# A diffusion step's expert stage on one core: one loop body for all sixteen experts, and a pass ahead of them that jumps over the body

## What is computed

```python
aff = jax.nn.softmax((h @ w_router).astype(jnp.float32), axis=-1)
gate, idx = lax.top_k(aff.transpose(0, 2, 1), cap)        # 64 latent and 16 context tokens for each expert
xs = jax.vmap(lambda hb, ib: hb[ib])(h, idx)
a = jnp.einsum('becd,edf->becf', xs, w1)
b = jnp.einsum('becd,edf->becf', xs, w3)
y = jnp.einsum('becf,efd->becd', jax.nn.silu(a) * b, w2) * gate[..., None]
```

## Time and profile before

| | us |
|---|---|
| median of 3 runs | 2695.71 |
| lowest and highest of them | 2691.11, 2699.36 |
| the profiled execution: its time | 2696.3 |
| its span in the trace | 2694.5 |
| experts of layer 0, from PE's first block to the end of its last | 865.6 to 1338.3 |
| experts of layer 1 | 2186.9 to 2661.3 |
| PE busy, share of the span | 94% |

### The profile page before, as it was taken

The page is one execution under the profiler, slowest core; times in us unless marked ns, Lnnn a source line. Parts: engine busy times, 40 slices in busy tenths (PEclk is TensorE's granted clock), DMA queues, the critical chain, the costliest instruction groups (busy, mean ns, idle before and its releaser), DMA issues.

```text
span 2694.5 us, 79955 instructions
## 1 busy us (share of the span) xinstructions
PE 2520.7 (94%) x31456; PEld 1918.2 (71%) x31456; DVE 1164.1 (43%) x2031; ACT 814.8 (30%) x3454; POOL 961.5 (36%) x2976
## 2 busy tenths in 40 slices
PE   6999999999997999999889999999999969999995
PEld 3555676666755899888746566766666559988885
DVE  3998534555426111111278874345644341111114
ACT  3112223434214343333021132334331143433320
POOL 2374223232201255445535632133221014554444
PEclk9999999999999999999999999999999979999998
DMA  8332311112336899999723322111242249999993
GB/s 329 114 146 94 113 60 50 67 63 103 148 125 256 327 427 428 427 427 427 331 102 125 132 95 92 61 66 53 105 167 74 113 159 404 427 427 427 428 427 148
DMA packets 45134, 572.39 MB, mean 212 GB/s; under 512 B 5248, under 2 KB 7424, under 8 KB 9600
## 3 DMA queue, kind: packets, MB, share of 16 engines
q1 hardware_dynamic: 42336, 553.67, 50.7%
q10 hardware_dynamic: 2592, 16.38, 1.5%
HBM read 561.11 MB, written 8.91 MB: 212 GB/s over the span
## 4 chain that ended last, share of the span: by engine, by line
PE 67%; DMA 20%; DVE 10%; issue 2%; ACT 1%; DVEq 0%; POOL 0%; POOLq 0%; ACTq 0%
PE ps L511 50%; DMA ring<-in_w_exp 18%; PE ps L678 6%; DVE region_b L1707 5%; PE ps L933 3%; DMA ring<-in_w_last 2%; PE ps L899 1%; PE ps L882 1%; PE ps L870 1%; PE ps L1043 1%; DVE region_r L1996 1%; DVE rstd L1621 0%; DVE region_r L1995 0%; DVE region_r L1999 0%; PE ps L785 0%
## 5 line engine op out<-in xcount | busy, mean ns | idle before, releaser
L2321 POOL TENSOR_TENSOR region_m<-region_m,region_r 128x8 f32 x2416 | 424.1, 217 | 542.8 <-DVE region_r L2036 489.3
L511 PE MATMUL ps<-hT,ring 128*128 128x320 f32 (+2 forms) x1440 | 429.0, 440 | 8.4 <-ACT hT L1221 8.2
L2329 ACT ACTIVATE region_b<-hT 128x8 f32 x2400 | 290.6, 204 | 270.4 <-DVE region_r L2049 158.9
L511 PEld LDWEIGHTS ps<-hT,ring 128*128 128x128 f32 x1440 | 256.2, 191 | 145.0 <-issue 65.7
L511 PE MATMUL ps<-region_r,ring 128*64 128x80 f32 x7812 | 287.3, 233 | 22.2 <-DMA ring<-in_w_exp 19.3
L511 PEld LDWEIGHTS ps<-region_r,ring 128*64 128x64 f32 x7812 | 278.3, 137 | 28.9 <-DMA ring<-in_w_exp 25.8
L1707 DVE SCALAR_TENSOR_TENSOR region_b<-region_b,params 128x655 f32<-128x655 f32 x240 | 277.6, 1157 | 8.5
L511 PE MATMUL ps<-region_b,ring 128*128 128x320 f32 (+1 forms) x812 | 191.7, 373 | 0.5 <-DMA ring<-in_w_last 0.5
L511 PE MATMUL ps<-region_r,spare 128*64 128x80 f32 x4032 | 152.6, 237 | 27.9 <-DVE region_r L2331 18.1
L2167 POOL TENSOR_TENSOR params<-ring 128x512 f32<-128x512 f32 x32 | 41.9, 1310 | 372.2 <-DMA ring<-in_w_pair 370.7
L511 PEld LDWEIGHTS ps<-region_r,spare 128*64 128x64 f32 x4032 | 147.7, 140 | 32.0 <-DVE region_r L2331 18.6
(11 more groups left out here) (291 smaller groups left out, 3778.8 us busy)
## 6 DMA issues: line engine op xcount, KB each, us to landing
region_b<-in_w_exp SPq DMA_DIRECT2D x60, 2048.0 KB, 25.2
ring<-in_w_exp SPq DMA_DIRECT2D x60, 2048.0 KB, 25.3
ring<-in_w_mix SPq DMA_DIRECT2D x39, 2048.0 KB, 8.1
region_x<-in_w_exp SPq DMA_DIRECT2D x30, 2048.0 KB, 25.2
spare<-in_w_exp SPq DMA_DIRECT2D x30, 2048.0 KB, 25.3
ring<-in_w_pair SPq DMA_DIRECT2D x32, 1536.0 KB, 6.4
ring<-in_w_ada SPq DMA_DIRECT2D x4, 2048.0 KB, 10.3
x_store<-region_m ACTq DMA_DIRECT2D x2, 2560.0 KB, 10.6
```

Of the source, the lines that this page charges most:

```text
L511: ins = pe.matmul(*args, **kw)
L2321: last = eng.tensor_tensor(x[:, :, token], x[:, :, token], y_gated[e % 2][:, :, c:c + 1], ALU.add)
L2329: last = eng.activation(into[:, :, c:c + 1], h[:, :, token], ACT.Copy)
```

## The change

The loop body becomes one expert: w1, w3, w1, w3, w2, w2 of the same expert, blocks 6e to 6e+5, with six slots (4, 1, 5, 2, 3, 0) from the first block on. The blocks written out ahead of the loop and behind it are gone. `pe.Fori(0, NE + 1)` makes seventeen passes, and each block stands in a `pe.If(e)` of its own: in the pass e = 0 PE jumps over all six. The wait for `xs_first` is inside the first of them. In w2 half 0, PE takes the first half of the rows of all four column groups before it waits for the second product of silu and b. y has two banks. The gates are laid and spread for one expert at a time, by a matmul in each pass. ACT gathers 48 columns ahead of `silu(2e)` and 32 after it. DVE finds the context tokens ahead of its last latent round, so that after the last result 8 columns are left to gather (ACT 3, POOL 2, DVE 3) and 16 are gathered before. PE does all of `next_ada` ahead of `turn_affinities(2)`. The four `in_w_ada` blocks go to slots 7, 6, 3 and 0 and are issued at the pairs 11 to 13 and behind `br_read`, where blocks of experts were. DVE no longer helps with expert 14. Cut to its core:

```diff
-FIRST_BLOCKS, LOOP_BLOCKS, LAST_BLOCKS = 4, 3 * (HALVES - 2), 2
...
-ADA_SLOTS = (0, 1, 2, 0)
-FIRST_SLOTS = (7, 3, 6, 0)
-LOOP_SLOTS = (4, 1, 5, 2, 7, 3)
-AHEAD = 8
+ADA_SLOTS = (7, 6, 3, 0)
+EXP_SLOTS = (4, 1, 5, 2, 3, 0)
...
-        take(FIRST_SLOTS[_n] if _n < FIRST_BLOCKS else LOOP_SLOTS[(_n - FIRST_BLOCKS) % EXP_BLOCKS], expert=(_l, _n))
+        take(EXP_SLOTS[_n % EXP_BLOCKS], expert=(_l, _n))
...
-        GATE_BANKS = [(PS[1][:, 1, 0:6 * CAP], 0, 6), (PS[3][:, 0, 0:6 * CAP], 6, 6), (PS[3][:, 1, 0:4 * CAP], 12, 4)]
-        gates_laid = sq[0:NE, 0:NE * CAP].rearrange("p (e c) -> p e c", e=NE)
+        gates_laid = sq[0:NE, 0:CAP]
+        a_ps, b_ps = PS[0][:, 0, 0:HC], PS[0][:, 1, 0:HC]
+        y_banks, gate_bank = [PS[1][:, 0, 0:HC], PS[2][:, 0, 0:HC]], PS[1][:, 1, 0:CAP]
...
-                    if (name, p) == ("pair", 11):
-                        load_expert(0)
-                    if (name, p) == ("pair", 12):
+                    if l == 0 and (name, p) == ("pair", 11):
+                        load_next_ada(0)
+                    if l == 0 and (name, p) == ("pair", 12):
                         need("o_ready", 2 * PAIRS)
                         sp.wait_ge(kv_stored, 2 * 16 * (l + 1))
-                        load_expert(2)
+                        load_next_ada(1)
                     if (name, p) == ("pair", 13):
                         need("br_step", 56)
-                        load_expert(1)
+                        load_next_ada(2) if l == 0 else load_expert(4)
                     if (l, n) == (0, 0):
                         sp.dma_start(first_block, a["w_conv0"]).then_inc(first_in, 16)
                 need("br_read", 32)
-                load_expert(4)
+                load_expert(0)
+                load_next_ada(3) if l == 0 else load_expert(5)
+                load_expert(1)
+                need("ctx_out_done", 2)
+                load_expert(2)
+                load_expert(3)
                 if l == 0:
-                    for n, b in enumerate(NEXT_ADA[:SLOTS]):
-                        load(BLOCK_AT[1][b], a["w_ada"][n])
-                else:
-                    load_expert(3)
+                    load_expert(4)
                     load_expert(5)
-                need("ctx_out_done", 2)
-                load_expert(6)
-                if l == 0:
-                    for at, b in enumerate(NEXT_ADA[SLOTS:], SLOTS):
-                        load(BLOCK_AT[1][b], a["w_ada"][at])
-                    load_expert(5)
-                load_expert(7)
-                if l == 0:
-                    load_expert(3)
-                for n in range(AHEAD, EXP_BLOCKS * NE):
+                for n in range(EXP_BLOCKS, EXP_BLOCKS * NE):
...
+                        if m == 0 and pending:
+                            last.then_inc(slot_used[pending.pop(0)], 1)
...
-                next_ada(("turn", 1), ("rows", 2))
+                next_ada(("turn", 1), ("rows", 2), ("turn", 2), ("rows", 3), ("turn", 3))
                 turn_affinities(2)
-                next_ada(("turn", 2), ("rows", 3), ("turn", 3))
-                a_ps, b_ps = PS[0][:, 0, 0:HC], PS[0][:, 1, 0:HC]
-                y_ps = PS[1][:, 0, 0:HC]
...
+                def spread_gates(e):
+                    need("gates_laid", e)
+                    pe.matmul(gate_bank, ones[0:NE, :], gates_laid, start=True, stop=True).then_inc(S["gates_wide"], 1)
+                def expert_step(w, ps, moving, m, k, start):
+                    for at in range(0, P, WCOLS):
+                        ins = pe.matmul(
+                            ps[at:at + WCOLS, m * CAP:(m + 1) * CAP],
+                            w[:, k, m * P + at:m * P + at + WCOLS], moving[:, k, :],
+                            start=start, stop=k == KC - 1, tile_position=(0, at), skip_group_check=True)
+                    return ins
+                def up_block(n, turns, ps, done):
                     w = weights(EXP_AT[l] + n, turns)
                     for m in range(4):
                         for k in range(KC):
...
+                            ins = expert_step(w, ps, xs, m, k, k == 0)
                     ins.then_inc(S[done], 1)
...
-                need("xs_first", 3)
-                up_blocks(0, 0, 0, True)
-                spread_gates()
-                up_blocks(1, 2, 0, False)
-                with pe.Fori(1, NE) as e:
-                    need("xs_ready", e)
-                    up_blocks(2 * e, FIRST_BLOCKS, e - 1, False)
-                    down_block(2 * e, FIRST_BLOCKS + 2, e - 1)
-                    up_blocks(2 * e + 1, FIRST_BLOCKS + 3, e - 1, False)
-                    down_block(2 * e + 1, FIRST_BLOCKS + 5, e - 1)
-                for b in range(LAST_BLOCKS):
-                    need("act_ready", HALVES)
-                    expert_block(FIRST_BLOCKS + LOOP_BLOCKS + b, 0, last_banks[b], act_last, "y_done")
...
+                def down_block(n, e, half):
+                    w = weights(EXP_AT[l] + n, e - 1)
+                    need("y_copied", 2 * e + half)
+                    for part in range(2):
+                        if part and not half:
+                            need("b_used", 2 * e + 2)
+                        for m in range(4):
+                            for k in range(part * KC // 2, (part + 1) * KC // 2):
+                                ins = expert_step(w, y_banks[half], act, m, k, (m, k) == (0, 0))
+                    ins.then_inc(S["y_done"], 1)
+                assert not pending
+                if l + 1 < LAYERS:
+                    pe.wait_ge(S["ada_part_in"], ADA_BLOCKS * (l + 1) + ADA_EARLY[l + 1])
+                with pe.Fori(0, NE + 1) as e:
+                    for half in range(2):
+                        with pe.If(e):
+                            if half == 0:
+                                need("xs_first", 3)
+                                need("xs_ready", e)
+                            need("sil_ready", 2 * e + half)
+                            up_block(2 * half, e - 1, a_ps, "a_done")
+                        with pe.If(e):
+                            need("b_used", 2 * e + half)
+                            up_block(2 * half + 1, e - 1, b_ps, "b_done")
+                    for half in range(2):
+                        with pe.If(e):
+                            if half == 0:
+                                spread_gates(e)
+                            down_block(4 + half, e, half)
...
+                need("index_ready", 8)
+                take_slots(nc, sc, mybir.EngineType.Activation, index, 0, h, xs, CAPL, CAPL + 8)
                 need("index_ready", 9)
-                take_slots(nc, sc, mybir.EngineType.Activation, index, 0, h, xs, CAPL, CAPL + 5).then_inc(S["xs_first"], 1)
+                take_slots(nc, sc, mybir.EngineType.Activation, index, 0, h, xs, CAPL - 8, CAPL - 5).then_inc(S["xs_first"], 1)
                 def silu(i):
                     need("a_done", i + 1)
                     if i >= 2:
-                        need("act_ready", i // 2 * 2)
-                    sc.activation(sil[i % 2], PS[0][:, 0, 0:HC], ACT.Silu).then_inc(S["sil_ready"], 1)
+                        need("b_used", i + 1)
+                    sc.activation(sil[i % 2], a_ps, ACT.Silu).then_inc(S["sil_ready"], 1)
                 def next_slots(e, c0, c1):
-                    if e < NE:
-                        return take_slots(nc, sc, mybir.EngineType.Activation, index, e, h, xs_next, c0, c1)
...
-                for e in range(1, NE):
+                    return take_slots(nc, sc, mybir.EngineType.Activation, index, e, h, xs_next, c0, c1)
+                sc.sem_inc(S["sil_ready"], 2)
+                for e in range(NE):
                     if e < NE - 1:
-                        need("xs_ready", e)
-                        next_slots(e + 1, 0, CAP // 2)
+                        if e:
+                            need("xs_ready", e + 1)
+                        next_slots(e + 1, 0, PARKED)
                     silu(2 * e)
                     if e < NE - 1:
-                        next_slots(e + 1, CAP // 2, CAP).then_inc(S["xs_parked"], 1)
+                        next_slots(e + 1, PARKED, CAP).then_inc(S["xs_parked"], 1)
                     silu(2 * e + 1)
...
+                    if c == CAPL - 8:
+                        need("aff_turned", 2)
+                        link(v.tensor_copy(affW[:, LAT:TOK], PS[2][0:NE, 1, 0:CTX]), "aff_copied")
+                        for ctx_c in range(CAPL, CAP, 8):
+                            top(ctx_c, CAPL, LAT, TOK, CAPC)
+                        link(v.tensor_scalar(best_raw[:, CAPL:CAP], best_raw[:, CAPL:CAP], float(LAT), None, ALU.add),
+                             "index_ready")
                     top(c, 0, 0, LAT, CAPL)
...
+                take_slots(nc, v, mybir.EngineType.DVE, index, 0, h, xs, CAPL - 3, CAPL).then_inc(S["xs_first"], 1)
+                def lay_gates(e):
+                    if e:
+                        need("gates_wide", e)
```

(65 more changed lines are left out.)

83 lines of the change are left out of this document (15 added, 68 removed).

## The result

| | us |
|---|---|
| before, median of 4 runs | 2696.38 |
| after, median of 4 runs (lowest, highest) | 2822.31 (2817.48, 2826.27) |
| ratio, with its 95% interval | 1.0468 (1.0445 to 1.0492) |
| span of the profiled execution, before and after | 2694.5, 2820.2 |

What follows compares the result with a forecast made beforehand. The experts' weight stream, 5.04 us per block, and its start bound the kernel. Layer 0's +9.7 and layer 1's +1.4 sum to +11.1 us: 2707.4 against the profiled 2696.3, 0.6 less against the median, 2707; range 2680 to 2717.

Steps and rivals of the forecast that it cites:

- the jump pass and the stream: Both expert loops: fetches put first blocks at 879.0 and 2193.7; block 6's issue to last start 457.1 us; sum +11.1 us.
- No stall of over 1 us: Sign of being right: in the expert loops' first pass of work, no "issue" pauses of over 1 us.
- what a fetch costs: Jump pass: five packets waited for per layer, one behind the other, 3.8 us each, 4.5 for layer 0's first.
- the old body of six blocks stays held; the new one is longer by some tens of instructions: PE's expert loop: argument against code being fetched again in every pass, which would cost 400 us in all.
- rival 3: Expert loop body outgrows what PE holds: every pass fetches again, 13 us per pass, 400 us in all; chance 0.04.
- The rule of the skill: Jump pass: prefetch is sequential only; a taken branch to a block not held forces a fetch before execution goes on.
- The shorter wait for the first block: Ahead of the experts: fewer columns left to gather, 0.9 us, starts 864.6 and 2186.0 without the jump; worth nothing behind it.

Runs made afterwards that it cites:

- e1: The changed kernel with 40 long-met waits (about 20 PE instructions) ahead of layer 1's loop, so its body lies in seven packets: 2706.95 us, ratio 1.0038.
- e2: The kernel before with 472 long-met waits (236 instructions) ahead of layer 1's experts, moving its loop's head to a packet's end: 2753.32 us, ratio 1.021.
- e5: The changed kernel with 74 more wait instructions ahead of layer 0's loop, so layer 0's body touches eight packets and layer 1's seven: 2846.94 us, ratio 1.0599.
- e7: The changed kernel with 56 more wait instructions ahead of layer 0's loop, both bodies in seven packets, layer 0's ending near its seventh's end: 2704.99 us, ratio 1.0036.
- e8: The changed kernel without the empty first pass and jumps, layer 1's body kept where it touches eight packets: 2795.44 us, ratio 1.0364.
- e3: The changed kernel without the empty first pass and jumps, layer 1's loop moved by 20 instructions into seven packets: 2693.38 us, ratio 0.999.
- e4: The changed kernel with three jumps over pairs of blocks instead of six, layer 1's loop moved by 20 instructions: 2700.08 us, ratio 1.0024.
- e6: The changed kernel with layer 1's loop moved by 40 waits and a second empty pass added in layer 1: 2710.26 us, ratio 1.0052.

## Why the prediction was wrong, step by step

**Right in kind and size: the jump pass and the stream.** From block 6's issue, at 882.37 in the SP timeline, to the last start of layer 0, 1339.44, it is 457.07 us; forecast 457.1. No stall of over 1 us is left in layer 0's first pass. PE comes to its pass 2.7 us earlier than I had it, since all of this execution ahead of the experts was 2.7 us earlier than in the profile before; from there to the first block it is 19.5 us, and my sum had 20.0. e1, the change with the misplacing taken out, has 2706.95 against the forecast's 2707: layer 0 starts its first and last block at 878.26 and 1342.43 (forecast 879.0, 1343.4), and layer 1's last block starts at 2668.19, where 2658.1 and layer 0's 9.7 make 2667.8.

**Right by errors that cancel: what a fetch costs.** I had five fetches of 3.8 us in each layer. q8 has six packets in layer 0's pause, at 859.7, 862.9, 866.2, 869.4, 872.4 and 875.4, one each 3.2 us and not 3.8; the last starts 0.4 us ahead of the first block, less than the 0.94 that a packet takes, so five seem to be waited for. The first starts 3.4 us behind PE's arrival, where I had at most 1.2, and that makes up for the cheaper ones. Layer 1 of e1 has seven, 2184.8 to 2204.3, and by the same reading waits for six: 21.8 us for my 19.3, while PE came there 1.3 us earlier than forecast and the stretch to the last block was 0.8 shorter. I had counted blocks; what counts is the packets that the body touches, less what is held on arrival. In the kernel after, layer 1's pause is 27.4 us with nine packets, 2183.2 to 2207.3: there the body is lost for the first time as soon as PE jumps back from the pass that only fetched it.

**Failed: "the old body of six blocks stays held; the new one is longer by some tens of instructions", so 0.04 for rival 3, and it was left out of the range.** So the sum gave refetching nothing, and it is 115 of the 126 us. The step asked whether the body's length fits. What decides is how many packets it touches, and that is its length and its place: 1560 instructions are seven packets from slot 172 and eight from slot 250. The 15 instructions that the body grew by weren't needed for it: e2's old body, moved, is lost too. The earlier trace rows showed a loop that is held; they couldn't show with how much to spare, and I read a "yes" as a margin. Nor did I ask for each layer by itself, though the two loops are compiled to two places. e1, e5, e7 and e8 show it with the same body in both places, and e2 with the old body. Rival 3's price per pass that fetches, 13 us against 13.5, came out right by luck: it was seven packets of 6.2 us against 30 us of work, and it is nine packets and a pause of 11.8 to 13.4 us at the back edge. Its count was wrong: eight such passes, in one layer, and not all of both.

By the sum of the parts: the stretch ahead of the first block of layer 1 is 22.9 us later than before (2209.78 against 2186.92), of which 8.0 are there already at the last matmul ahead (2181.99 against 2173.98); from there to the last block's start another 103.7 (573.5 against 469.8): together 126.5, less 0.8 behind it: 125.7, the difference of the spans.

**The rule of the skill.** The Trainium skill, "Runtime: NRT & Kernel Launch", section "Instruction fetch mechanics", was right that a jump to a packet not held waits for it. The same section gives TensorE a buffer of 128 KiB in blocks of 16 KiB, which makes eight blocks. Runs here agree with it as an order of size, and put the edge at seven packets touched. That the eighth is kept for the packet fetched ahead would explain it. The packet that starts 0.3 to 0.4 us ahead of the first block (in both layers of e1 and in layer 0 of the kernel after), too late to be waited for, and the nine packets of each refetch, one more than the body touches, fit that; no run tests it. The Trainium skill, "Advanced Engine Details and Errata", section "ISA Cache", with its two lines, doesn't hold for PE in this kernel: seven stay held through a layer.

**Not settled**: why only every second pass fetches (every fourth or second in e2, at times two in a row in e5), and why the pause at the back edge, 11.8 to 13.4 us, is two fetches long (7.3 and 4.4 us in e5) while further packets of the same pass cost 0.3 to 2 us each. One reading is that those come ahead of PE while it works and compete with the weights.

**A better version.** None. e3 is at 0.999 with an interval up to 1.0: within what a measurement of this kernel can tell from no change. The shorter wait for the first block that the rest of the change brings (863.11 against 865.55) is paid for by a block at the lower clock, 7.23 us against 5.89, and the stalls stay.

## What to carry to other kernels

A hardware loop whose body comes near to what its engine holds has to be judged by the packets it touches in the compiled program, for each copy of the loop: a few instructions ahead of it can be worth 4% of the time (e1 against the kernel after), and every timing of a change to such a kernel is then a timing of its placement too. So look first at whether q8 has packets in the later passes of each layer, and if it has, move the loop by some idle instructions before anything else is concluded. A pass that only fetches code pays one fetch after another, 3.2 us a packet here, and is worth it only where PE is idle for that long anyway.

## What the runs showed of the hardware that I had not expected

- PE keeps seven packets of 16 KB through sixteen passes (q8 has none in 340 us), and with eight touched it loses them all, nine packets for each refetch: 45 packets in 390 us, 13.5 us per pair of passes. The step from one to the other is 18 instructions or fewer (e7 against e5), 14 in e8 against e3.
- Code that is jumped over by pairs of packets is fetched all the same (e4: 68 packets, no stall in the first pass of work).
- A pass of six jumps over held code isn't free: 2.7 us (e6).
- After a pause at the back edge the next block runs 5.9 to 7.5 us in place of 4.6. The granted clock falls in the pause, as in the second of these windows of the kernel after, which lies almost wholly in the pause of 13.39 us (the last three columns are clock, DMA share and GB/s):

```profile
2330.00:2345.00 15.00, 13.40 (x375) 13.06 (x370) 3.01 (x7) 5.92 (x49) 2.19 (x13) 1.00 1.01 430
2345.00:2357.00 12.00, 0.21 (x4) 0.22 (x6) 0.00 (x0) 0.00 (x0) 10.95 (x64) 0.61 0.71 292
```
